# Attention scaling shared between VectorE and GpSimd, linear attention's end by row tile, and a later place for one weight chunk at three borders

## The reference

```
layer 1: h = LN(a*x + dsa_mixer(x));  h = LN(a*h + mlp(h))
    # 16 heads of 64, causal; a small indexer picks at most 128 keys
    # of each query: p = softmax(q k / 8 over the picked keys)
layer 2: h = LN(a*h + gla_mixer(h));  h = LN(a*h + mlp(h))
    # gated linear attention, 4 heads, state 128 x 256 per head:
    # state = exp(b_last)*state + (k*exp(b_last - b))^T v
    # o = intra + (q*exp(b)) state;  o = o * rsqrt(mean(o^2) + eps) * g_norm
    # y = (o * silu(r)) @ w_o
block 2: x = x + g1*(attention | bidirectional mLSTM)(mod(rms(x))) @ w_out
         x = x + g2*((silu(h @ w_gate) * (h @ w_up)) @ w_down)
    # attention without a mask, 8 heads of 64; the scale and shift
    # of mod() come from c @ w_ada
mlp(x) = square(relu(x @ w_up)) @ w_down          # 1024 -> 4096 -> 1024
```

## Time and profile before

| what | us |
|---|---|
| median of three runs | 2035.85 (2034.58 to 2042.59) |
| the profiled execution | 2042.75 |
| its span | 2040.7 |
| PE busy | 1909.1 (94%) |
| DVE busy | 1176.8 (58%) |
| ACT busy | 737.3 (36%) |
| POOL busy | 179.2 (9%) |
| mean granted clock of PE, as a share of full | 0.962 |
| load of an up projection's chunk, issue to landing | 5.7 |
| from one 512-wide matmul to the next at full clock (border x1) | 0.23 |
| DVE's statistics of half a row (line 1867, border x1) | 0.69 |

### The profile page before, as it was taken

How to read it: one execution, slowest core, us unless ns; L and a number is a source line. 1 busy time by engine, 2 the same in 40 slices (tenths; PEclk the granted TensorE clock), 3 DMA queues, 4 the chain that set the end, 5 groups by cost and what they waited for, 6 DMA issues and landing times.

```text
span 2040.7 us, 23111 instructions
## 1 busy us (share of the span) xinstructions
PE 1909.1 (94%) x9196; PEld 1532.5 (75%) x9196; DVE 1176.8 (58%) x2155; ACT 737.3 (36%) x1147; POOL 179.2 (9%) x176
## 2 busy tenths in 40 slices
PE   7978799999999999979999999988899799999997
PEld 5764488888888878867888888766555688888886
DVE  3894458654555587456754545766765653433438
ACT  3435434322222443453322323255544443222221
POOL 0016600000000035000000000000053000000000
PEclk9998899999999999989999999999899899999999
DMA  5120043543445021113434333221000412323321
GB/s 180 56 83 1 1 145 105 169 143 124 141 146 165 22 83 42 62 63 103 145 104 144 103 124 112 76 63 63 21 1 1 155 42 83 116 90 104 103 83 42
DMA packets 116715, 184.06 MB, mean 90 GB/s; under 512 B 7120, under 2 KB 71632, under 8 KB 113536
## 3 DMA queue, kind: packets, MB, share of 16 engines
q1 hardware_dynamic: 115216, 177.77, 26.4%
q0 software_dynamic: 1392, 4.82, 0.8%
HBM read 180.47 MB, written 2.10 MB: 89 GB/s over the span
## 4 chain that ended last, share of the span: by engine, by line
PE 70%; DVE 17%; ACT 6%; issue 3%; POOL 2%; DMA 1%; DVEq 0%; SPq 0%; ACTq 0%
PE bank L577 9%; PE bank L579 9%; PE bank L578 9%; PE bank L756 6%; PE bank L755 6%; PE bank L754 6%; DVE wl L1789 3%; PE bank L553 2%; PE bank L555 2%; PE bank L554 2%; DVE gb L2148 1%; PE bank L812 1%; PE bank L796 1%; ACT wh L1185 1%; DVE m L2146 1%
## 5 line engine op out<-in xcount | busy, mean ns | idle before, releaser
L1789 DVE TENSOR_TENSOR wl<-raw,wh 128x2048 fp32r<-128x2048 f32 (+1 forms) x143 | 321.4, 2253 | 212.2 <-ACT wh L1185 212.0
L1185 ACT ACTIVATE wh<-raw 128x2048 fp32r<-128x2048 f32 (+1 forms) x143 | 266.9, 1883 | 266.7 <-PE bank L756 90.5
L577 PE MATMUL bank<-xh,wh 128*128 128x512 f32 (+2 forms) x880 | 348.6, 396 | 2.2 <-DVE wl L1789 2.2
L578 PE MATMUL bank<-xh,wl 128*128 128x512 f32 (+2 forms) x880 | 347.3, 395 | 0.0
L579 PE MATMUL bank<-xl,wh 128*128 128x512 f32 (+2 forms) x880 | 347.2, 395 | 0.0
L756 PE MATMUL bank<-wh,ul 128*128 128x512 f32 x592 | 230.4, 389 | 0.0
L755 PE MATMUL bank<-wl,uh 128*128 128x512 f32 x592 | 230.4, 389 | 0.0
L754 PE MATMUL bank<-wh,uh 128*128 128x512 f32 x592 | 230.4, 389 | 0.0
L577 PEld LDWEIGHTS bank<-xh,wh 128*128 128x128 f32 (+2 forms) x880 | 165.7, 188 | 42.7 <-DVE wl L1789 3.1
L579 PEld LDWEIGHTS bank<-xl,wh 128*128 128x128 f32 (+2 forms) x880 | 165.4, 188 | 39.0
L578 PEld LDWEIGHTS bank<-xh,wl 128*128 128x128 f32 (+2 forms) x880 | 165.7, 188 | 38.3
(11 more groups left out here) (352 smaller groups left out, 3199.0 us busy)
## 6 DMA issues: line engine op xcount, KB each, us to landing
raw<-in_mlp_w_up SPq DMA_DIRECT2D x32, 1024.0 KB, 5.7
raw<-in_mlp_w_down SPq DMA_DIRECT2D x32, 1024.0 KB, 5.1
raw<-in_w_ada SPq DMA_DIRECT2D x24, 1024.0 KB, 5.0
raw<-in_b_w_in SPq DMA_DIRECT2D x12, 1024.0 KB, 5.3
raw<-in_w_in SPq DMA_DIRECT2D x11, 1024.0 KB, 5.3
raw<-in_w_gate SPq DMA_DIRECT2D x11, 1024.0 KB, 5.4
raw<-in_w_up SPq DMA_DIRECT2D x11, 1024.0 KB, 5.4
raw<-in_w_down SPq DMA_DIRECT2D x10, 1024.0 KB, 5.0
```

The costliest lines, as they stand in the source:

```text
L577: pe.matmul(o, H[:, k, c], xh[:, k, :], start=k == 0, stop=False)
L578: pe.matmul(o, L[:, k, c], xh[:, k, :], start=False, stop=False)
L1185: act.activation(slots[slot_of[i]][0][:, 0:n], raw[:, i % NRAW, 0:n], ACT.Copy).then_inc(*s_high.up(i))
L1789: dve.tensor_tensor(L[:, 0:n], raw[:, i % NRAW, 0:n], H[:, 0:n].bitcast(F), ALU.subtract).then_inc(*s_low.up(i))
```

## The change

- **Scaling in attention.** A function `by_pool(key, i)` says who scales a row. In A the rows of 128 and 256 stay on POOL, those of 384 and 512 are scaled by DVE directly behind their reciprocal, with a wait for it; in B the even i stay on POOL and the odd i go to DVE. PE waits for the one or the other.
- **End of linear attention.** Three ticks instead of two behind each row tile in r0 and in r1's first chunk; the jobs are drained before r1's second chunk, in which no ticks are. The first half of r is silu'd in row pairs at the start of r1's second chunk; the second half gets its Silu straight from PSUM; DVE gates by tile and half; PE transposes y's rows 0 and 1 behind tiles 2 and 3 of that chunk; ACT makes xh of y's first pair at tile 2, DVE xl of it behind the gating of tile 2; the take that prepares `first_by_pairs`' second chunk follows these. For chunk 3 the factor KD, which only feeds the state, is no longer made.
- **Borders x1, x2, x3.** `Cursor.reach` prepares without using. The first take of `cross` looks 2 ahead instead of n_groups + 1; the other chunks are prepared by `reach` behind row 1 (before row 2) on ACT, and behind `scale(1)` (before row 2's columns) on DVE.

```diff
@@ -147,14 +147,18 @@
...
         self.used = i + 1
-        ahead = i
+        self.reach(prepare, look)
+        return i
+    def reach(self, prepare, look):
+        ahead = self.used - 1
         for _ in range(look):
...
             self.make(prepare)
-        return i
@@ -438,6 +442,10 @@
...
         rel = [A[:, 11264 + 512 * i:11776 + 512 * i] for i in range(4)]
+        def by_pool(key, i):
+            return i // 2 % T < 2 if key == "A" else i % 2 == 0
         PB1 = [rz[:, i // 2, 512 * (i % 2):512 * (i % 2) + 512] for i in range(8)]
@@ -533,11 +541,14 @@
...
-            def gemm_tok(key, n, x_key, ticks=0):
+            def gemm_tok(key, n, x_key, ticks=0, last_ticks=None, after=None):
                 for t in range(T):
...
                 while k0 < 8:
+                    if k0 and last_ticks is not None:
+                        drain(jobs)
+                        ticks = last_ticks
                     i = cur.take(skip)
@@ -559,6 +570,8 @@
...
                             banks.drop((key, t))
+                            if after:
+                                after(t)
                         tick(jobs, ticks)
@@ -791,7 +804,7 @@
...
                     w.wait_ge(*banks.free((key, "p", i), s_act.sem))
-                    w.wait_ge(*s_pool.at((key, "norm", i)))
+                    w.wait_ge(*(s_pool if by_pool(key, i) else s_step).at((key, "norm", i)))
                     for kb in range(n // P):
@@ -948,14 +961,14 @@
...
                         yield
-                        if f and c < 3:
+                        if f and c < 2:
                             dec = decays(c + 1)
...
                     yield
-                    if c < 3:
+                    if c < 2:
                         next(dec)
@@ -972,11 +985,12 @@
...
                 gemm_tok(("v", n), 512, "x2", 2)
-            for n in range(2):
-                gemm_tok(("r", n), 512, "x2", 2)
-            drain(jobs)
-            for t in range(2):
-                turn_row("y", t, gv[:, t], s_step.at(("y", t)))
+            def turned_y(t):
+                if t > 1:
+                    turn_row("y", t - 2, gv[:, t - 2], s_step.at(("y", t - 2)))
+            gemm_tok(("r", 0), 512, "x2", 3)
+            gemm_tok(("r", 1), 512, "x2", 3, 0, turned_y)
             first_by_pairs("o2", "y", lambda t: gv[:, t], lambda t: s_step.at(("y", t)))
@@ -1210,10 +1224,15 @@
...
-            def gemm_tok(key, n, evict, ticks=0):
+            def gemm_tok(key, n, evict, ticks=0, last_ticks=None, first=None):
                 k0 = 0
                 while k0 < 8:
+                    if k0 and last_ticks is not None:
+                        drain(jobs)
+                        ticks = last_ticks
                     nk = chunks[cur.take(high)][1]
+                    if k0 and first:
+                        first()
                     for t in range(T):
@@ -1273,7 +1292,7 @@
...
             def cross(x_key, gain, shift, n_groups):
-                cur.take(high, n_groups + 1)
+                cur.take(high, 2)
                 cur.take(high, 0)
@@ -1283,6 +1302,7 @@
...
                 row(1)
+                cur.reach(high, n_groups)
                 row(2)
@@ -1456,13 +1476,12 @@
...
-            gates_in = []
             def silu_in():
-                while gates_in:
-                    t = gates_in.pop(0)
-                    w.wait_ge(*s_act.at(("r", t, 1)))
-                    act.activation(rz[:, t, :], rz[:, t, :], ACT.Silu).then_inc(*s_act.up(("silu", t)))
+                for p in range(2):
+                    v = rz[:, 2 * p:2 * p + 2, 0:512]
+                    w.wait_ge(*s_act.at((("r", 0), 2 * p + 1)))
+                    act.activation(v, v, ACT.Silu).then_inc(*s_act.up(("silu", 2 * p, 0), ("silu", 2 * p + 1, 0)))
@@ -1471,6 +1490,8 @@
...
                 act.activation(QE, bb[:, :, c * P:(c + 1) * P], ACT.Exp, scale=0.0625).then_inc(*s_act.up(("qe", c)))
+                if c == 3:
+                    return
                 w.wait_ge(*s_step.at(("kdiff", c)))
@@ -1489,9 +1510,7 @@
...
                             dec = decays(c + 1)
-                            next(dec)
-                        if c == 3:
-                            silu_in()
+                            next(dec, None)
                         w.wait_ge(*s_mm.at(("go", c, f)))
@@ -1522,15 +1541,15 @@
...
                 def evict_r(t, ps):
-                    act.activation(rz[:, t, n * 512:(n + 1) * 512], ps, ACT.Copy).then_inc(*s_act.up(("r", t, n)))
-                    banks.read[("r", n), t] = s_act.at(("r", t, n))
-                    if n:
-                        gates_in.append(t)
-                gemm_tok(("r", n), 512, evict_r, 2)
-            drain(jobs)
-            silu_in()
+                    if n == 0:
+                        copy_to((("r", n), t), rz[:, t, 0:512], ps)
+                        return
+                    act.activation(rz[:, t, 512:1024], ps, ACT.Silu).then_inc(*s_act.up(("silu", t, 1)))
+                    banks.read[("r", n), t] = s_act.at(("silu", t, 1))
+                    if t == 2:
+                        half("y", 0, GNC, None)
+                gemm_tok(("r", n), 512, evict_r, 3, 0 if n else None, silu_in if n else None)
             cur.take(high)
-            half("y", 0, GNC, None)
             half("y", 1, GNC, None)
@@ -1809,9 +1828,12 @@
...
-            def gemm_tok(key, evict=None, ticks=0):
+            def gemm_tok(key, evict=None, ticks=0, last_ticks=None):
                 k0 = 0
                 while k0 < 8:
+                    if k0 and last_ticks is not None:
+                        drain(jobs)
+                        ticks = last_ticks
                     nk = chunks[cur.take(low)][1]
@@ -1873,7 +1895,7 @@
...
             def cross(row_key, x_key, n_groups, evict):
-                cur.take(low, n_groups + 1)
+                cur.take(low, 2)
                 cur.take(low, 0)
@@ -1889,6 +1911,8 @@
...
                     scale(t)
+                    if t == 1:
+                        cur.reach(low, n_groups)
                 for k in range(4):
@@ -2051,6 +2075,10 @@
...
                             dve.reciprocal(rc[:, hd, t:t + 1], sm[:, hd, t:t + 1]).then_inc(*s_step.up((key, "rc", i)))
+                            if not by_pool(key, i):
+                                pb = bufs[i % NB][:, 0:P * (t + 1) if causal else SEQ]
+                                w.wait_ge(*s_step.at((key, "rc", i)))
+                                dve.tensor_scalar(pb, pb, rc[:, hd, t:t + 1], None, ALU.mult).then_inc(*s_step.up((key, "norm", i)))
                     g = u - 2
@@ -2226,10 +2254,10 @@
...
-            def gated(t):
-                w.wait_ge(*s_act.at(("silu", t)))
+            def gated(t, n):
+                w.wait_ge(*s_act.at(("silu", t, n)))
                 w.wait_ge(*s_step.at(("grs", t)))
-                for q in range(4):
+                for q in (2 * n, 2 * n + 1):
                     o = gv[:, t, q * 256:(q + 1) * 256]
@@ -2241,10 +2269,13 @@
...
                 bl = bb[:, :, c * P + 127:c * P + 128]
-                dve.tensor_tensor(KD, bl.broadcast_to([P, 4, P]), bb[:, :, cs], ALU.subtract).then_inc(*s_step.up(("kdiff", c)))
+                if c < 3:
+                    dve.tensor_tensor(KD, bl.broadcast_to([P, 4, P]), bb[:, :, cs], ALU.subtract).then_inc(*s_step.up(("kdiff", c)))
                 yield
...
                 dve.tensor_tensor(QE, QE, gq[:, :, cs], ALU.mult).then_inc(*s_step.up(("qe", c)))
+                if c == 3:
+                    return
                 w.wait_ge(*s_act.at(("kd", c)))
@@ -2294,16 +2325,15 @@
...
                 gemm_tok(("v", n), None, 2)
-            for n in range(2):
-                gemm_tok(("r", n), None, 2)
-            drain(jobs)
-            gated(0)
-            gated(1)
+            gemm_tok(("r", 0), None, 3)
+            gemm_tok(("r", 1), None, 3, 0)
+            for t in range(T):
+                gated(t, 0)
+                gated(t, 1)
+                if t == 2:
+                    for k in range(8):
+                        split("y", 0, k)
             cur.take(low)
-            for k in range(8):
-                split("y", 0, k)
-            gated(2)
-            gated(3)
             for k in range(8):
@@ -2686,6 +2716,8 @@
...
                 for i in range(nheads * T):
+                    if not by_pool(key, i):
+                        continue
                     hd, t = 2 * (i // (2 * T)) + i % 2, i // 2 % T
```

## The result

The changed kernel takes 2007.57 us (median of four, 2002.08 to 2009.05) beside 2038.24 us for the kernel before in the same comparison. The ratio is 0.9844, with a 95% interval of 0.9814 to 0.9873: 32 us less, 26 to 38. The prediction was 2024, 12 less, with a range that began at 2008. The direction was right, the size was not: it was two and a half times as large.

What follows compares the result with a forecast made beforehand. PE, busy 1909.1 of 2040.7 us, bounds the kernel, so at most 131 us of waits can go. Terms −12 + 3 − 11.5 − 0.5 + 9 = −12, from the median 2035.85 to 2024 us; range 2008 to 2038.

Steps and rivals of the forecast that it cites:

- A, predicted −12: Attention A: long rows scaled on DVE instead of POOL shorten the loop of hand-overs; −12 us, likely −20 to −6.
- a clock that is up a little more often than 0.81: Attention A: granted clock rises slightly; 1.8 us of the −12.
- the loop: worked out as 10.8 us: Attention A: full-clock period falls from 11.95 to 10.8 us, 1.15 less; seven periods give 8.0.
- Rival (a): Attention A gains more, loop near DVE's busy-time floor of 8.95 us and clock back: −20 to −26 total; chance 0.18.
- Rival (c): Waits move: A −5, linear attention's end gains only 7; −2 in all, 2034 us; chance 0.17.
- B, predicted +3: Attention B: odd rows scaled on DVE, little wait to win, DVE possibly held by POOL; +3 us, ends −4 and +12.
- if POOL is first each time, DVE is held for the 1.56: Attention B: DVE waits out POOL's scaling, 2.0 us per unit, 32 us in sixteen units.
- the free end (−1 to −4): Attention B: DVE's added scaling delays nothing, so only the small gain of −1 to −4 us remains.
- late next: End of linear attention, remaining delays: tile 1's turning 0.9, y's first low half 0.7, second chunk's low half 1.7, clock 1.0; 4.3.
- The end of linear attention, predicted −12: Pause filled with r's second chunk: net −11.5 us, bounds −14 and −7; chunk 3's unused state factor dropped, −0.5.
- The term for the faster ticks: Linear attention: three ticks per row tile leave a third less matmul to hide the scan chain behind; +1.5 us.
- The borders, predicted +9: Borders x1, x2, x3: second weight chunk made behind row 1 delays row 2; +9 us, bounds +7 and +12.

Runs made afterwards that it cites:

- filler kernel: Kernel before, with 128 useless identity transposes put in front of PE's wait for the scaled 384 rows in attention A; ratio 0.9964.
- doubled kernel: Kernel before with only attention A's long rows moved to DVE, each scaled row multiplied once more by 1.0; ratio 0.9957.
- run with POOL first: Changed kernel, but in attention B DVE scales the odd row behind its copy from PSUM; 1999.43 us (two executions).

## Why the prediction was wrong

**A, predicted −12, did −23.5.** By its own sign the prediction is wrong here: A shrank by more than 20. The mechanism was right: POOL's block of four rows was what PE waited for. Two terms were mis-sized. The filler kernel separates them, as it has the old loop at full clock. These are the six repeating periods, and then the drained end, over the same instructions of before, of the filler kernel and of the changed kernel (columns of the earlier trace rows):

```profile
170.20:248.70 78.50, 60.95 (x356) 34.34 (x357) 38.90 (x170) 39.70 (x125) 51.25 (x49) 0.85 0.00 1
170.75:242.50 71.75, 62.95 (x453) 39.05 (x453) 38.88 (x170) 39.77 (x126) 51.24 (x49) 1.00 0.00 1
169.47:230.67 61.20, 51.60 (x357) 29.22 (x357) 48.26 (x199) 40.15 (x127) 18.08 (x24) 1.00 0.00 1
```

```profile
248.70:262.00 13.30, 11.80 (x52) 8.13 (x53) 3.09 (x4) 4.74 (x5) 5.43 (x5) 0.62 0.14 44
242.50:253.30 10.80, 8.58 (x57) 6.37 (x58) 2.64 (x4) 4.29 (x5) 5.51 (x5) 1.00 0.12 45
230.67:239.40 8.73, 7.85 (x52) 5.92 (x53) 4.39 (x10) 4.84 (x8) 1.27 (x2) 1.00 0.16 52
```

The first term is the clock. I counted 1.8 us for "a clock that is up a little more often than 0.81". Measured it is 6.8 us in the six periods and 2.5 in the end, 9.3 together. Both periods, 13.0 and 11.95 us, stood in the earlier trace rows had 0.81 over the stretch and 1.00 in that one period. I reckoned the new loop from the full-clock period and so left the clock's part of the old loop out of the sum. The second is the loop: worked out as 10.8 us, measured as 10.20, so 1.76 instead of 1.15 per period; it repeats six times, not the seven that I counted, which makes 10.6 instead of 8.0. The end without its clock is 2.1, where I had 2.2. What is left, 1.6 us, lies in the first period, for which I had no term. How large the clock's part is depends on the execution it is compared with: in two other kernels with A as before the clock was 0.75 and the stretch 3.6 to 3.9 us longer. Rival (a), with the floor of 8.95 us and the returning clock, named both; the measured loop stands between its floor and mine. Rival (c) was added up wrong: its parts make −0.5, not −2.

The price of a scaling was wrong as well, with little effect. I took 360 and 426 ns and called them scalings by one value per row. The changed kernel shows 420 and 487:

```profile
L2081 DVE TENSOR_SCALAR rz<-rz,att 128x512 f32<-128x512 f32 x16 | 7.8, 487 | 0.6
L2081 DVE TENSOR_SCALAR rz<-rz,att 128x384 f32<-128x384 f32 x16 | 6.7, 420 | 0.6
```

and the doubled kernel shows why: there the multiplication by the constant 1.0 took 427 and 360. The rows I read were of that kind, without a second operand; those of line 2127, which read a value per row, would have been the right ones.

**B, predicted +3, did −6.1 (−6.1 alone).** The step that failed is the bound "if POOL is first each time, DVE is held for the 1.56", which pulled the middle up. The run with POOL first shows no hold, so of the 32 us nothing exists, and the free end (−1 to −4) was the right one. What goes beyond it is clock, and not the change's. These are the same instructions of PE in before, in the kernel with the end of linear attention alone (B as before), and in the one with B alone:

```profile
1465.00:1590.00 125.00, 113.86 (x606) 70.19 (x607) 76.63 (x260) 58.17 (x158) 49.63 (x32) 0.94 0.00 1
1449.57:1572.48 122.91, 111.72 (x606) 69.16 (x607) 76.72 (x260) 58.32 (x158) 49.72 (x32) 0.96 0.00 1
1458.54:1577.48 118.94, 110.37 (x606) 69.06 (x607) 84.01 (x276) 57.41 (x158) 29.37 (x16) 0.96 0.00 1
```

The first two differ by 2.1 us of clock without any change in B; at equal clock the change gives 4.0, of which 2.6 are idle time of PE. Another kernel with B as before (the one with the ticks alone) was at 0.97 and took 121.27 us, which leaves 2.3; so the places alone bound the change's worth between 2.3 and 6.1, and the ten executions of the kernel with B alone (7 us less, 4 to 10) say that it is a gain.

The rule of the Trainium skill that I weighed ("SBUF — State Buffer", section "Who interferes with whom": the one that issues first has the shared ports for its whole instruction) doesn't agree with the 0.49 us beside a POOL row 0.47 us old. It is stated for a two-port mode, and no row names DVE's mode; but 128 columns more cost the scaling 67 ns, and DVE's copy from PSUM 140 ns (551 and 691 ns for 384 and 512), so the scaling runs at twice the rate of the copy. Where both start at once, POOL takes 0.27 us longer, less than the 0.49 of DVE's scaling; whether it is held there for a part of it, no run shows. The measurement decides. That DVE's add took 0.88 instead of 0.40 us beside POOL's stands: those were other operations, with two tensors from SBUF.

**The end of linear attention, predicted −12, did −14.6 by place and −12 by time.** The wait of 11.23 is gone, and of what was to be "late next" the first low half of y waits 0.9 (I had 0.7) and the second chunk's low half 1.1 (I had 1.7). The term for the faster ticks had the wrong sign: −5 instead of +1.5. The total hardly shows it, since that gain and that of the new end share one wait; what ticks alone take off it, 6.3 us, the new end doesn't have to take.

**The borders, predicted +9, did +10.2 (alone +11.0, by time +12).** The chain was right to a few tenths. At x1 of the changed kernel:

```profile
272.70 0.16 DVE L1907 SCALAR_TENSOR_TENSOR small<-mv,small 128x1 f32<-128x1 f32 x1
272.89 1.25 ACT L1300 ACTIVATE h<-h,small 128x1024 f32<-128x1024 f32 x1 [4.25 <-DVE small L1907]
274.05 1.90 ACT L1199 ACTIVATE wh<-raw 128x2048 fp32r<-128x2048 f32 x1
...
276.05 2.29 DVE L1808 TENSOR_TENSOR wl<-raw,wh 128x2048 fp32r<-128x2048 f32 x1 [1.98 <-ACT wh L1199]
278.25 0.68 DVE L1978 SCALAR_TENSOR_TENSOR h<-h,bank 128x512 f32<-128x512 f32 x1
...
283.04 0.16 DVE L1907 SCALAR_TENSOR_TENSOR small<-mv,small 128x1 f32<-128x1 f32 x1
...
286.06 0.55 PE L691 MATMUL bank<-xh,wh 128*128 128x256 f32 x1 [3.76 <-DVE xl L1882]
```

From row 1's scale to row 2's are 10.34 us; I had 10.5. PE waits 3.76 us; I had 3.8. What was too small is the clock behind the pause: 0.9 us for x1 and x2 together, where it is 2.8 (5.1 and 5.8 behind waits of 3.8 and 4.3), with 0.68 granted in the ten microseconds shown above. At x3 one pause took the other's place, as predicted.

In sum: the largest error is one term, the granted clock around PE's pauses, which I wrote down as a remainder: 9.3 us instead of 1.8 in A, 2.8 instead of 0.9 at the borders. The second is a bound taken for real in B, and the third the loop of A, with its 2.6 us. The sum came out 20 us short because the errors of A and B point the same way; that of the borders, 1 us, points the other.

## What to carry to other kernels

Where PE pauses often and the page shows a clock below 1, price a shorter wait twice: the wait itself, and the matmul time of the stretch brought to full clock (compare the stretch's mean period with its best full-clock period, and do so in several executions: the clock of an unchanged stretch was 0.75 in one and 0.85 in another). Moving work on an in-order engine behind one row and before the next costs the whole work at the next row unless that engine idles there; a place that helps where a transfer is late (x3) can harm where it isn't (x1, x2). And look for the price of an operation in rows with the same kind of operands, not only the same size.

## What the runs showed of the hardware

- 128 useless transposes in PE's waits made attention A 8.5 us faster: clock 0.97 instead of 0.81, every period 11.96 us.
- DVE's scaling of 128x512 from SBUF to SBUF takes 487 ns with a value per row and 427 ns with a constant; beside a POOL operation that began 0.47 us before it takes 490 ns, and POOL's stays at 1562 ns. When both start at once DVE takes 487 ns and POOL 1836 ns, in all 16 units.
- A pause of PE of 3.8 us at x1 costs 5.1 us in all, with a clock of 0.68 over the ten microseconds around it (x2: 5.8 us lost with a wait of 4.3 at most).
- The same instructions of attention A, unchanged, took 107.5 us at a mean clock of 0.85, 110.2 at 0.82 and 114.1 at 0.75 in the executions of three kernels (B alone, before, ticks alone).
